# A decoder block's head: h in blocks of 128 rows, and the last adaLN row of the scale taken by TensorE

## The reference, cut to what matters

```
mod = silu(c) @ w_ada + b_ada                 # (1, 1024) @ (1024, 6144) -> six vectors of 1024
sh_a, sc_a, gt_a, sh_f, sc_f, gt_f = split(mod, 6)
h    = rms_norm(x, g_attn) * (1 + sc_a) + sh_a # x is (512, 1024)
proj = h @ w_in                                # (512, 1024) @ (1024, 3072), cut into the q, k, v of
                                               # differential and of stick-breaking attention
x    = x + gt_a * (concat(A, B) @ w_out)       # A, B: the two attentions
x    = x + gt_f * hier_moe(rms_norm(x, g_ffn) * (1 + sc_f) + sh_f)   # 4 groups of 8 experts, top 2
```

## Time and profile before

| | |
|---|---|
| median of 3 runs | 619.59 us (618.88 to 620.04) |
| profiled execution | 618.37 us |
| its span in the trace | 616.4 us |
| PE busy | 543.3 us, 88% |
| DVE, ACT, POOL busy | 297.9, 184.3, 79.1 us |
| mean granted clock of TensorE | 0.986 |

### The profile page before, as it was taken

One profiled execution on the slowest core, in us unless ns is written; L12 is line 12 of the kernel. 1 busy time (PEld: TensorE's weight loads), 2 busy tenths in 40 slices (PEclk: granted clock), 3 DMA queues, 4 the chain that ended last, 5 costly groups with the idle time before them and its releaser, 6 DMA issues.

```text
span 616.4 us, 7800 instructions
## 1 busy us (share of the span) xinstructions
PE 543.3 (88%) x3018; PEld 342.6 (56%) x3018; DVE 297.9 (48%) x523; ACT 184.3 (30%) x328; POOL 79.1 (13%) x101
## 2 busy tenths in 40 slices
PE   1689999999988999999999848899998999878797
PEld 1577768778766666665446524455544445434443
DVE  4988674366889736661032664233222223312216
ACT  5265562343454458872042211000000000000002
POOL 8132100000000000000041111112111111200000
PEclk9989999999999999999999869999999999999999
DMA  8987855495253074002920497999999999999957
GB/s 335 400 256 261 310 189 213 157 387 207 68 206 103 1 288 190 1 2 77 425 112 34 188 366 261 409 417 421 420 419 419 419 418 422 419 420 423 401 233 290
DMA packets 42626, 169.28 MB, mean 275 GB/s; under 512 B 7848, under 2 KB 9896, under 8 KB 30308
## 3 DMA queue, kind: packets, MB, share of 16 engines
q1 hardware_dynamic: 32356, 140.81, 57.3%
q0 software_dynamic: 9104, 25.95, 11.9%
q10 hardware_dynamic: 1136, 2.11, 0.9%
HBM read 160.74 MB, written 16.25 MB: 287 GB/s over the span
## 4 chain that ended last, share of the span: by engine, by line
PE 62%; DMA 13%; DVE 9%; SPq 8%; ACT 4%; issue 2%; DVEq 0%; POOLq 0%; ACTq 0%
PE banks L1833 11%; PE banks L1712 9%; PE banks L1853 5%; DMA qkT<-in_w_dram 5%; DMA obuf<-in_w_dram 4%; PE banks L1547 4%; PE banks L1549 4%; PE banks L1548 4%; PE banks L1664 3%; DMA stage<-in_w_in_dram 3%; PE banks L1648 2%; PE banks L1541 2%; PE banks L1539 2%; PE banks L1540 2%; SPq L455 2%
## 5 line engine op out<-in xcount | busy, mean ns | idle before, releaser
L859 ACT ACTIVATE work<-banks 128x256 f32<-128x256 f32 x16 | 6.1, 384 | 198.4 <-PE banks L1833 198.4
L1853 PE MATMUL banks<-stage,work 128*64 128x512 f32 x168 | 58.3, 598 | 6.3 <-ACT work L861 6.3
L1833 PE MATMUL banks<-qkT,work 128*64 128x256 f32 x272 | 61.5, 381 | 0.3 <-DMA stage<-in_w_dram 0.3
L1712 PE MATMUL banks<-stage,mixT 128*128 128x512 f32 x128 | 56.2, 594 | 0.0
L1356 DVE TENSOR_TENSOR work<-banks,gates 128x1024 f32<-128x1024 f32 x15 | 18.4, 1225 | 72.7 <-PE banks L1853 72.7
L1350 DVE TENSOR_TENSOR work<-work,banks 128x256 f32<-128x256 f32 x16 | 6.7, 422 | 87.4 <-ACT work L859 87.4
L1833 PE MATMUL banks<-hT,work 128*64 128x256 f32 x192 | 43.2, 381 | 2.8 <-DMA qkT<-in_w_dram 2.8
L1549 PE MATMUL banks<-hT_hi,w_lo 128*128 128x512 f32 x112 | 43.8, 391 | 0.0
L899 DVE SCALAR_TENSOR_TENSOR mixT<-stage,small,mixT 128x1024 f32<-128x1024 f32 x32 | 41.0, 1282 | 0.6
L1547 PE MATMUL banks<-hT_hi,w_hi 128*128 128x512 f32 x96 | 40.4, 421 | 0.0
L1712 PEld LDWEIGHTS banks<-stage,mixT 128*128 128x128 f32 x128 | 24.0, 190 | 28.9 <-issue 28.9
(11 more groups left out here) (304 smaller groups left out, 1156.4 us busy)
## 6 DMA issues: line engine op xcount, KB each, us to landing
stage<-in_w_dram SPq DMA_DIRECT2D x31, 1024.0 KB, 20.3
qkT<-in_w_dram SPq DMA_DIRECT2D x23, 1024.0 KB, 23.8
stage<-in_w_ada_dram POOLq DMA_DIRECT2D x16, 1024.0 KB, 5.7
hT<-in_w_dram SPq DMA_DIRECT2D x12, 1024.0 KB
stage<-in_w_in_dram SPq DMA_DIRECT2D x5, 2048.0 KB, 11.2
val<-in_w_dram SPq DMA_DIRECT2D x10, 1024.0 KB
mixT<-in_w_dram SPq DMA_DIRECT2D x10, 1024.0 KB
alibi<-in_w_dram SPq DMA_DIRECT2D x5, 1024.0 KB
```

The lines of the kernel that those rows point to most:

```text
L1712: ins = mm(banks[:, w % 5, :], mixT[:, k, t * P:(t + 1) * P], wv[:, k % 4, half * 512:(half + 1) * 512], start=(k == 0), stop=(k == KD - 1))
L1833: ins = mm(banks[half * C:(half + 1) * C, 2, up * F:(up + 1) * F], heT[:, r, k * P + half * C:k * P + (half + 1) * C], ws[2 * place + half ...
L1853: ins = mm(banks[half * C:(half + 1) * C, 4 + 2 * r + col, :], geT[:, fc * P + half * C:fc * P + (half + 1) * C], w2s[2 * place + half][:, ...
```

## The change

Six things are done together.

1. w_in's row k*128 + p goes to partition p, instead of row p*8 + k. So block k of hT is now columns k*128 to k*128 + 127 of xn, which x_T reads as they lie, and block k of shift and scale is 128 columns of `acc` as they lie. The turned last row (L906) goes for these two vectors.
2. The scale's row 7 isn't added by VectorE. TensorE takes it as column sums of its own: the raw w_ada row block as weights, with cs[:, 7] in place of ones. SP's second w_in piece waits for `scale_row` too.
3. The two biases and the gain come as 24 rows of 128 into a corner of mixT, and one matmul with the identity puts them, transposed, into bank 0, where the column sums are added to them. VectorE copies 16 columns out and multiplies (1 + scale) by the gain.
4. VectorE does mod before w_rest(0), w_rest(1) after the hT_hi blocks, and hT_lo(0) between hT_hi(4) and hT_hi(5). ScalarE does w_round(1) after the hT blocks. `first_pair` takes chunk 1's w_hi products first, then its w_lo ones, and the hT_lo ones in the order 0, 6, 7, 1 to 5.
5. x tile 3 is loaded between the scale's quarters 1 and 2. TensorE transposes it ahead of the fillers.
6. Fillers: 16 when `scale_used` is 6, ahead of both groups of column sums, and 14 after `mod_a`.

```diff
-HEAD_FILLERS = ((KD // 2, 16), (KD - 1, 12))
+HEAD_FILLERS = (16, 14)
...
+        mod_rows = by_col[0:3 * KD, 0, 0:P]
...
-        in_v = w_in.rearrange("l (p k) n -> (l p) k n", k=KD)
+        in_v = w_in.rearrange("l (k p) n -> (l p) k n", p=P)
...
             for i in range(4):
+                if i == 2:
+                    x_tile(NT - 1)
                 ada_quarter(scale_w, SCALE_A, i)
-            x_tile(NT - 1)
...
-                    sp.wait_ge(scale_used, KD)
+                    sp.wait_ge(scale_used, KD - 1)
+                    sp.wait_ge(scale_row, 1)
...
-            act.dma_start(b_col[:, 0:2, :], b_cols_v[:, SHIFT_A:SCALE_A + 1, :]).then_inc(mod_params_in, 16)
-            act.dma_start(g_col[:, 0, :], g_attn.rearrange("l (p k) -> (l p) k", k=KD)).then_inc(mod_params_in, 16)
+            act.dma_start(mod_rows[0:2 * KD, :], b_rows_v[SHIFT_A * KD:(SCALE_A + 1) * KD, :]).then_inc(mod_params_in, 16)
+            act.dma_start(mod_rows[2 * KD:3 * KD, :], g_attn.rearrange("l (k p) -> (l k) p", p=P)).then_inc(mod_params_in, 16)
...
             w_round(0)
-            w_round(1)
             act.wait_ge(mod_a, 1)
             for k in range(KD):
                 act.wait_ge(xT_done, k + 1)
                 a.activation(hT[:, k, :], ...).then_inc(hT_raw, 1)
+            w_round(1)
             w_round(2)
...
-            first_sums(0, shift_w, shift_used)
-            first_sums(1, scale_w, scale_used)
+            first_sums(0, shift_w, shift_used, KD)
+            first_sums(1, scale_w, scale_used, KD - 1)
...
-            w_rest(0)
-            dve.wait_ge(mod_params_in, 32)
             dve.wait_ge(col_a, 1)
-            v.tensor_tensor(mod[:, 0, :], banks[:, 0, 0:8], b_col[:, 0, :], ALU.add)
-            link(v.tensor_tensor(mod[:, 1, :], banks[:, 0, 8:16], b_col[:, 1, :], ALU.add))
-            v.scalar_tensor_tensor(out=mod[:, 1, :], in0=mod[:, 1, :], scalar=1.0, in1=g_col[:, 0, :],
+            link(v.tensor_copy(mod[:, 0:2, :].rearrange("p v k -> p (v k)"), banks[:, 0, 0:2 * KD]))
+            v.scalar_tensor_tensor(out=mod[:, 1, :], in0=mod[:, 1, :], scalar=1.0, in1=banks[:, 0, 2 * KD:3 * KD],
                                    op0=ALU.add, op1=ALU.mult).then_inc(mod_a, 1)
             dve.wait_ge(mod_a, 1)
-            w_rest(1)
+            w_rest(0)
             for k in range(KD):
                 dve.wait_ge(hT_raw, k + 1)
                 v.tensor_copy(hT_hi[:, k, :], hT[:, k, :]).then_inc(hT_hi_ready, 1)
-            for k in range(6):
-                ...
+                if k == KD // 2:
+                    hT_rest(0)
+            w_rest(1)
+            for k in range(1, 6):
+                hT_rest(k)
...
+            for t in range(NT - 1):
+                x_tile_T(t)
+            pe.wait_ge(mod_params_in, 32)
+            mm(banks[:, 0, 0:3 * KD], mod_rows, ident[0:3 * KD, 0:3 * KD], start=True, stop=False, skip_group_check=True)
+            pe.wait_ge(shift_used, KD)
+            column_sums(0, acc[:, 0, :], ones[:, 0:1])
+            x_tile_T(NT - 1)
+            pe.wait_ge(scale_used, KD - 2)
+            head_fill(HEAD_FILLERS[0])
+            pe.wait_ge(first_in[7], 16)
+            column_sums(1, scale_w[1][:, 3, :], cs[:, KD - 1:KD]).then_inc(scale_row, 1)
+            pe.wait_ge(scale_used, KD - 1)
+            column_sums(1, acc[:, 1, :], ones[:, 0:1]).then_inc(col_a, 1)
+            pe.wait_ge(mod_a, 1)
+            head_fill(HEAD_FILLERS[1])
             pe.wait_ge(hT_raw, 1)
...
             def first_pair():
+                pe.wait_ge(w_split, 1)
+                for k in range(KD):
+                    pe.wait_ge(hT_hi_ready, k + 1)
+                    mm(banks[:, 0, :], w_hi[:, k, 0:P], hT_hi[:, k, :], start=(k == 0), stop=False)
+                    mm(banks[:, 0, :], lo[:, k, 0:P], hT_hi[:, k, :], start=False, stop=False)
+                pe.wait_ge(w_hi_ready, 2)
+                for k in range(KD):
+                    mm(banks[:, 1, :], w_hi[:, k, P:2 * P], hT_hi[:, k, :], start=(k == 0), stop=False)
+                pe.wait_ge(w_split, 2)
+                for k in range(KD):
+                    mm(banks[:, 1, :], lo[:, k, P:2 * P], hT_hi[:, k, :], start=False, stop=False)
                 for c in range(2):
-                    for k in range(KD):
+                    for k in (0, 6, 7, 1, 2, 3, 4, 5):
```

More of the change, by code:

```diff
@@ L243, in hymba_block @@
         c_col, cs = cols(8), cols(8)
-        b_col = cols(32).rearrange("p (v k) -> p v k", v=4)
-        g_col = cols(16).rearrange("p (v k) -> p v k", v=2)
+        b_col = cols(16).rearrange("p (v k) -> p v k", v=2)
+        g_col = cols(8)
         mod = cols(32).rearrange("p (v k) -> p v k", v=4)
@@ L330, in hymba_block @@
         b_cols_v = b_ada.rearrange("l (v p k) -> (l p) v k", v=6, k=KD)
+        b_rows_v = b_ada.rearrange("l (v k p) -> (l v k) p", v=6, p=P)
         def piece(n):
@@ L351, in hymba_block @@
         params = [
-            (b_col[:, 2:4, :], b_cols_v[:, SHIFT_F:SCALE_F + 1, :]),
-            (g_col[:, 1, :], g_ffn.rearrange("l (p k) -> (l p) k", k=KD)),
+            (b_col, b_cols_v[:, SHIFT_F:SCALE_F + 1, :]),
+            (g_col, g_ffn.rearrange("l (p k) -> (l p) k", k=KD)),
             (out_g[:, 0:1], diff_out_g.rearrange("l (p o) -> (l p) o", o=1)),
@@ L907, in last_by_col, with first_sums @@
                                               in1=turned(sums), op0=ALU.mult, op1=ALU.add)
-            def first_sums(v, w, used):
-                for k in range(KD):
+            def first_sums(v, w, used, rows):
+                for k in range(rows):
                     if k % 2 == 0:
                         dve.wait_ge(first_in[4 * v + k // 2], 16)
[L914 to L917, removed]
+                    accumulate(acc[:, v, :], w[k // 4][:, k % 4, :], k, k == 0).then_inc(used, 1)
                     dve.wait_ge(used, k + 1)
@@ L956, in w_rest, with hT_rest @@
                 v.tensor_tensor(lo, raw, hi.bitcast(F32), ALU.subtract).then_inc(w_split, 1)
-            w_rest(0)
-            dve.wait_ge(mod_params_in, 32)
             dve.wait_ge(col_a, 1)
-            v.tensor_tensor(mod[:, 0, :], banks[:, 0, 0:8], b_col[:, 0, :], ALU.add)
-            link(v.tensor_tensor(mod[:, 1, :], banks[:, 0, 8:16], b_col[:, 1, :], ALU.add))
-            v.scalar_tensor_tensor(out=mod[:, 1, :], in0=mod[:, 1, :], scalar=1.0, in1=g_col[:, 0, :],
+            link(v.tensor_copy(mod[:, 0:2, :].rearrange("p v k -> p (v k)"), banks[:, 0, 0:2 * KD]))
+            v.scalar_tensor_tensor(out=mod[:, 1, :], in0=mod[:, 1, :], scalar=1.0, in1=banks[:, 0, 2 * KD:3 * KD],
                                    op0=ALU.add, op1=ALU.mult).then_inc(mod_a, 1)
             dve.wait_ge(mod_a, 1)
-            w_rest(1)
+            w_rest(0)
+            def hT_rest(k):
+                dve.wait_ge(hT_hi_ready, k + 1)
+                v.tensor_tensor(hT_lo[:, k, :], hT[:, k, :], hT_hi[:, k, :].bitcast(F32),
+                                ALU.subtract).then_inc(hT_lo_dve, 1)
             for k in range(KD):
@@ L1460, in x_T, with x_tile_T @@
                 return nc.tensor.transpose(banks[:, XT_BANK[k], t * P:(t + 1) * P],
[L1461 to L1480, removed]
+                                           xn[:, t, k * P:(k + 1) * P], ident)
+            def x_tile_T(t):
                 pe.wait_ge(xn_ready, t + 1)
@@ L1485, in _, with head_fill, column_sums @@
                         ins.then_inc(xT_done, 1)
+            def head_fill(count):
+                for n in range(count):
+                    mm(banks[:, 0, 256:512], ones_bf[:], ones_bf[:].unsqueeze(1).to_broadcast([P, 2, P]),
+                       start=False, stop=True, skip_group_check=True)
+            def column_sums(v, rows, by):
+                for k in range(KD):
+                    ins = mm(banks[:, 0, 8 * v + k:8 * v + k + 1], rows[:, k * P:(k + 1) * P], by,
+                             start=False, stop=True, skip_group_check=True)
+                return ins
+            for t in range(NT - 1):
[13 more added lines that the diff above has]
+            head_fill(HEAD_FILLERS[1])
             pe.wait_ge(hT_raw, 1)
@@ L1554, in first_pair @@
                 lo = w_lo_parts[:, 0, :].rearrange("p (k n) -> p k n", k=KD)
-                for c in range(2):
-                    part = slice(c * P, (c + 1) * P)
-                    pe.wait_ge(w_split, c + 1)
-                    for k in range(KD):
-                        pe.wait_ge(hT_hi_ready, k + 1 if c == 0 else KD)
-                        mm(banks[:, c, :], w_hi[:, k, part], hT_hi[:, k, :], start=(k == 0), stop=False)
-                        mm(banks[:, c, :], lo[:, k, part], hT_hi[:, k, :], start=False, stop=False)
-                for c in range(2):
-                    for k in range(KD):
+                pe.wait_ge(w_split, 1)
[7 more added lines that the diff above has]
+                pe.wait_ge(w_split, 2)
+                for k in range(KD):
```

(3 more changed lines are left out.)

11 lines of the change are left out of this document (4 added, 7 removed).

## The result

| | before | after |
|---|---|---|
| median of 20 runs | 619.42 us | 622.32 us |
| ratio, 95% interval | | 1.0049 [1.0034, 1.0065] |
| profiled execution | 618.37 us | 620.86 us |
| its span | 616.4 us | 618.8 us |
| mod_a | 35.69 | 37.15 + 0.16 = 37.31 |

The new kernel is slower by 2.9 us (0.5%) in the medians and by 2.5 us in the profiled executions. The forecast was +2.1, and 621.7 for the median. The loss is all there at the end of the first pair: 2.62 us, against 2.4 of the whole span. Both profiled executions are fast ones of their kind, the one before by 1.0 us against its median and the one after by 1.5.

The account below looks back on a forecast made before the run. The prediction took TensorE's stream to bound the kernel, its start set by mod_a and the first pair. mod_a +1.9 and the pair +0.2 gave +2.1 us: 620.5 like for like, 621.7 as median, range 618.2 to 624.4.

Parts of the forecast that it names:

- The direction and the path: Head: late quarter 2, row 5, fillers and two groups of sums put mod_a at 37.6, 1.9 us later.
- Fillers low and sums high: TensorE ahead of mod_a: 16 fillers at the low clock, 3.54 us; two column-sum groups at the high one, 1.95 each.
- w_rest(1) behind GpSimd: VectorE behind mod_a: w_rest(1) waits for GpSimd's first subtraction, ends at +8.35; last hT_lo at +12.45, pair's end at +14.85.
- The first matmul comes 1.4 us later, which the pair can absorb: Behind mod_a: 14 fillers at the low clock take 3.0 us and delay the first matmul 1.4 us, without cost.
- The term was sized at 0.2: From mod_a to the first pair's end: 14.85 us instead of 14.63, 0.2 us later.
- (a): Scale transfers: row 5 is on time, quarter 2 not delayed; mod_a +0.4, in all +0.6, 620.2 us; chance 0.20.
- (b): TensorE's clock is up from the fillers to the first pair's end: 620.1 us, or 617.5 to 618.9; chance 0.26.
- (c): TensorE's clock stays low through both column-sum groups: +5.1 and +0.2, 624.9 us; chance 0.09.
- (d): The change moves nothing, as later stages do not follow the first pair's end: 619.6 us; chance 0.05.

Follow-up runs that it names:

- new order only: Kernel before with only the new order around mod_a and the new first_pair order, old transfers and fillers kept: 620.17 us, ratio 0.9993.
- second profile: The unchanged new kernel timed and profiled once more against the kernel before: 622.70 us, ratio 1.0040.
- tile 3 last: New kernel with x tile 3 loaded behind the scale's last quarter and transposed behind the column sums: 621.70 us, ratio 1.0049 to the kernel before.
- no late fillers: New kernel without the 14 fillers behind mod_a: 622.53 us, ratio 1.0047 to the kernel before.
- row 7 on VectorE: New kernel with the scale's eighth row added by VectorE and one group of column sums instead of two: 619.05 us, ratio 0.9995 to the kernel before.
- fillers early: New kernel with its 16 fillers ahead of x tile 3's transposes, waiting for nothing: 619.79 us, ratio 1.0004 to the kernel before.

## Why the prediction was right, point by point

**The direction and the path: right.** The terms for mod_a, as foretold and as the new kernel's profile has them: quarter 2 at 27.4, and 27.08; row 5 at 30.0, and 29.69; fillers from 30.06, and 29.75; last sum at 37.2, and 36.83; mod_a at 37.6, and 37.31. The 0.3 us that all of them are early is there at 18.12, ahead of the scale's rows (18.47 before). It isn't the change's: in the run with the new order only, which has the old transfers, the turned shift row also starts at 19.46 instead of 19.80. Against before, mod_a moved by 1.62, not 1.9. With the 0.35 of the head's start set aside it moved by 1.97, and the pair's end by 2.97 instead of 2.62, which is nearer to the 2.9 of the medians; that the one profile of before is late by chance is my reading, as there is no second one.

**Fillers low and sums high: roughly right.** I took 3.54, 1.95 and 1.95. Measured were 3.19, 1.84 and 2.35, and 2.86, 1.84 and 2.67 in the second profile. The sums are 7.4 each time, but that is luck: the clock went up before the fillers' end and down before the sums', and the two misses cancel.

**w_rest(1) behind GpSimd: right.** It took 1.95 instead of 1.22 us and ended at 43.78 + 1.95 - 37.31 = +8.42, against +8.35 foretold. In five profiles, all with mod_a at 35.3 or earlier, the pair took 14.92 to 14.94 us against +14.85 foretold. In the new kernel the last hT_lo was ready at +12.75 against +12.45, since the five behind w_rest(1) took 4.40 us; why they took 0.2 us more than in those five profiles is open. Without the late fillers this alone gave +15.14.

**"The first matmul comes 1.4 us later, which the pair can absorb": wrong.** This is the step that failed. I priced the 14 fillers at the low level, but the prediction's own numbers leave TensorE only 14.85 - 14.1 = 0.75 us of slack, half of the 1.4: worked through, they give about +15.5. I also left out that the four transposes stand behind the fillers rather than beside ScalarE's first blocks (1.06 us), and put the end of the first 16 matmuls at +6.45, which in the kernel before was +6.78 (42.47), seven of them having begun at the low level. The first matmul came 3.73 us behind mod_a, 2.0 later than before, and the 16 ended at 45.52, +8.21. hT_lo(5) was ready at 45.66 + 4.40 - 37.31 = +12.75, but TensorE reached the hT_lo products only at 49.15, +11.84, with 16 to go. TensorE, not VectorE, ended the pair, at +15.63 (+15.30 the second time). The term was sized at 0.2 and measured 1.0 and 0.7. Of that 0.5 is the pair as VectorE ends it (+15.14 without the fillers, against +14.63), and 0.5 and 0.2 are what TensorE's late start adds. With it the sum is 1.62 + 1.00 = 2.62, the profile's shift at that point.

**Rivals.** (a) The fillers started sooner only when tile 3 was put back, so quarter 2 was late as worked out. (b) The clock stayed up through both groups of sums only with other fillers. (c) It was low all through the sums in one profile of the run with tile 3 last, and in neither of the two of the new kernel. (d) The shift of 2.62 us arrived at the end as 2.4.

**What was not asked.** I treated the eighth row on TensorE as a given length. Its price, 1.8 us of TensorE against 1.3 of an idle VectorE, was in the sum, but that undoing it alone makes up the difference to before was seen only by doing it. It isn't the only edit that does: with the row left where it is, other fillers do it too (1.0004 and 0.9987). The loss is the queue on TensorE behind row 5, fillers and two groups of sums, and taking the fillers or one of the groups off it is enough. The blocks of 128 rows and the biases through TensorE were not tried by themselves.

## What to carry to other kernels

Work moved from one engine to another pays only if it doesn't lengthen what the receiving engine has to do between the last input and the result: here VectorE was freed 1.3 us earlier and then waited 5.93 for TensorE. Fillers that are to raise a clock are work in a queue; place them where the engine would idle whatever comes, not behind the input that the real work waits for, and price them at the lower clock (so placed, and with ten more, they brought mod_a from 37.31 to 33.98). A transfer moved forward delays those that it passes, and the engine that reads them shows it as a wait: 1.23 us here for half a megabyte, in every profile with tile 3 ahead of quarter 2, and none with it last.

## What the runs showed of the hardware

TensorE's clock had different levels at the same places in executions of one kernel: the 16 fillers took 3.19 and 2.86 us in two profiles, and 3.27 and 2.81 in kernels with the same work up to there. The view of the granted clock shows only 1.00 there. Column sums (one moving column for each 128x128 weights) took 0.11 us an instruction at the upper level and 0.21 at the lower, and in three kernels (new, no late fillers, fillers early) the clock fell while they ran back to back. Another such place, far from the change, blurs these comparisons: 16 matmuls of an expert near the end took 3.65 us in some executions and 5.35 in others, as in the new kernel and in the one with the new order only, here in this order:

```profile
583.80 3.65 PE L1875 MATMUL banks<-stage,work 128*64 128x512 f32 x16 [1.02 <-ACT work L865]
```
```profile
582.45 5.35 PE L1863 MATMUL banks<-stage,work 128*64 128x512 f32 x16 [1.01 <-ACT work L861]
```

The granted clock averages 1.00 over the first and 0.68 over the second. The 1.7 us between them is no part of the 2.5 between the profiled executions of before and after, which both have 3.65, but it is in four others (no late fillers, row 7 on VectorE, fillers early, new order only). It is why the stage's own end, and not the span, was read in each profile.
